# Differential stage: the second norm moved into the second values tile, wider spacing of a tile's steps, weight low halves that yield to two steps, and a swapped first output bank

## The reference, cut to what matters

```python
h = _rms(x, norm_g)                       # norm of the final-normed x: two norms in a row
q, k, v, g = split(h @ w_in)              # 8 heads of two 64-wide halves
qs = [_rope_partial(_rms(q[..., c, :], q_norm), pos) for c in range(2)]
ks = [_rope_partial(_rms(k[..., c, :], k_norm), pos) for c in range(2)]
a = probs(qs[0], ks[0]) - lam * probs(qs[1], ks[1])     # per block of 128 queries
o = _rms(a @ v, subln) * (1 - lambda_init) * silu(g)
return x + o @ w_out
```

## Time and profile before

| what | us |
|---|---|
| median of three runs | 2985.66 |
| the profiled execution | 2983.96 |
| its span, first to last instruction | 2982.0 |
| TensorE (matmul) busy | 2909.0 |
| VectorE busy | 1623.4 |
| ScalarE busy | 1069.4 |
| GpSimd busy | 391.2 |

### The profile page before, as it was taken

One profiled execution on the slowest core, in us unless ns is written; L12 is line 12 of the kernel. 1 busy time (PEld: TensorE's weight loads), 2 busy tenths in 40 slices (PEclk: granted clock), 3 DMA queues, 4 the chain that ended last, 5 costly groups with the idle time before them and its releaser, 6 DMA issues.

```text
span 2982.0 us, 35867 instructions
## 1 busy us (share of the span) xinstructions
PE 2909.0 (98%) x14832; PEld 2426.6 (81%) x14832; DVE 1623.4 (54%) x2239; ACT 1069.4 (36%) x1664; POOL 391.2 (13%) x262
## 2 busy tenths in 40 slices
PE   7999999999999999999999989999999999999999
PEld 6888888779888888888888879888888778678877
DVE  5554356565455533555346565555533666666774
ACT  4232234344333222323234444333223444434442
POOL 2000111120100001000011120100001312144330
PEclk8999999999999999999999999999999999999999
DMA  3333332233223323332332223333322222121211
GB/s 124 98 98 96 96 86 65 63 106 111 87 92 99 96 94 101 93 98 93 99 86 78 64 86 113 92 101 99 99 92 92 64 58 64 43 86 57 71 57 50
DMA packets 301361, 257.20 MB, mean 86 GB/s; under 512 B 10871, under 2 KB 299536, under 8 KB 301200
## 3 DMA queue, kind: packets, MB, share of 16 engines
q1 hardware_dynamic: 300880, 254.90, 27.9%
q0 software_dynamic: 320, 0.03, 0.0%
HBM read 252.79 MB, written 2.10 MB: 85 GB/s over the span
## 4 chain that ended last, share of the span: by engine, by line
PE 91%; DVE 5%; ACT 1%; issue 1%; POOL 1%; SPq 0%; DMA 0%; POOLq 0%; ACTq 0%; DVEq 0%
PE PS L1431 28%; PE PS L1433 28%; PE PS L1432 28%; PE PS L1673 2%; PE PS L1437 2%; DVE WL L2133 2%; PE PS L1678 1%; PE PS L1520 1%; PE PS L1629 1%; DVE PS L2393 0%; DVE AF L2548 0%; POOL SC L2658 0%; PE PS L1679 0%; DVE X L2395 0%; DVE SM L2466 0%
## 5 line engine op out<-in xcount | busy, mean ns | idle before, releaser
L2133 DVE TENSOR_TENSOR WL<-RAW,WH 128x1024 fp32r<-128x1024 f32 x480 | 624.0, 1306 | 583.9 <-ACT WH L1786 583.5
L1431 PE MATMUL PS<-XH,WL 128*128 128x512 f32 x2256 | 901.9, 400 | 9.0 <-issue 9.0
L1433 PE MATMUL PS<-XH,WH 128*128 128x512 f32 x2256 | 883.4, 392 | 0.0
L1432 PE MATMUL PS<-XL,WH 128*128 128x512 f32 x2256 | 882.4, 391 | 0.0
L1786 ACT ACTIVATE WH<-RAW 128x1024 fp32r<-128x1024 f32 x448 | 465.6, 1044 | 1036.7 <-PE PS L1433 1022.0
L1433 PEld LDWEIGHTS PS<-XH,WH 128*128 128x128 f32 x2256 | 425.6, 189 | 92.1
L1431 PEld LDWEIGHTS PS<-XH,WL 128*128 128x128 f32 x2256 | 426.7, 189 | 90.5 <-issue 9.7
L1432 PEld LDWEIGHTS PS<-XL,WH 128*128 128x128 f32 x2256 | 426.9, 189 | 81.6 <-issue 0.5
L1431 PE MATMUL PS<-AR,WL 128*128 128x512 f32 (+1 forms) x1216 | 465.6, 383 | 15.2 <-DVE X L2395 10.0
L1433 PE MATMUL PS<-AR,WH 128*128 128x512 f32 (+1 forms) x1216 | 462.0, 380 | 0.0
L1432 PE MATMUL PS<-AR,WH 128*128 128x512 f32 (+1 forms) x1216 | 461.4, 379 | 0.0
(11 more groups left out here) (244 smaller groups left out, 3067.1 us busy)
## 6 DMA issues: line engine op xcount, KB each, us to landing
RAW<-in_w_ffn_gu_dram SPq DMA_DIRECT2D x176, 512.0 KB, 3.5
RAW<-in_w_ffn_down_dram SPq DMA_DIRECT2D x80, 512.0 KB, 3.4
RAW<-in_w_mix_in_dram SPq DMA_DIRECT2D x48, 512.0 KB, 3.9
RAW<-in_w_xkv_dram SPq DMA_DIRECT2D x32, 512.0 KB, 3.4
RAW<-in_a_w_in_dram SPq DMA_DIRECT2D x32, 512.0 KB, 4.0
RAW<-in_w_mix_out_dram SPq DMA_DIRECT2D x16, 512.0 KB, 3.5
RAW<-in_w_xq_dram SPq DMA_DIRECT2D x16, 512.0 KB, 3.5
RAW<-in_w_xo_dram SPq DMA_DIRECT2D x16, 512.0 KB, 3.5
```

What stands on the lines that cost most here:

```text
L1431: pe.matmul(o, ll, rh, start=start, stop=False, skip_group_check=skip)
L1432: pe.matmul(o, lh, rl, start=False, stop=False, skip_group_check=skip)
L1433: return pe.matmul(o, lh, rh, start=False, stop=stop, skip_group_check=skip)
L2133: dve.tensor_tensor(l, raw_slot(n), F(h), ALU.subtract).then_inc(sg["wl"].up(n))
```

## The change

It orders the steps of the differential stage in another way; what is computed stays the same.

```diff
+        self.first = "drot", "dob"
...
-            self.later(10, "drot", k, "dr")
+            self.later(12, "drot", k, "dr")
             if w == "k":
-                self.later(12, "dkb", k, "dkb")
-            self.later(13, "dsin", k, "dsn", "dco")
+                self.later(13, "dkb", k, "dkb")
+            self.later(15, "dsin", k, "dsn", "dco")
             if w == "k":
-                self.later(15, "dkt", k, "dkt")
-            self.later(18, "dad", k, "dad", *(("dkm",) if w == "k" else ()), "eh")
-            self.later(22, "dlo", k, "el")
+                self.later(16, "dkt", k, "dkt")
+            self.later(20, "dad", k, "dad", *(("dkm",) if w == "k" else ()), "eh")
+            self.later(24, "dlo", k, "el")
...
-            self.later(11, "dot", ("o", t), "dot")
-            self.later(14, "dom", ("o", t), "dog", "dov", "oh")
-            self.later(19, "dol", ("o", t), "ol")
+            self.later(13, "dot", ("o", t), "dot")
+            self.later(16, "dom", ("o", t), "dog", "dov", "oh")
+            self.later(21, "dol", ("o", t), "ol")
...
         self.drain(self.flow(g))
+        g = self.flow(self.values(s, 1))
+        for _ in range(4):
+            next(g)
         self.add("norm2a", (s,), "na2", "ms2", "pw2", "ep2", "rcol2")
...
-        g = self.flow(self.values(s, 1))
         for _ in range(5):
             next(g)
         shape_up("q", 0)
...
             for c in range(2):
-                yield from self.tile(out[0], c, c, range(6))
+                yield from self.tile(out[0], 1 - c, c, range(6))
             yield from gated(7)
```

## The result

The change made the kernel slower: 2988.75 us, median of 22 runs (2985.96 to 2993.96), against 2983.81 for the kernel before in the same comparisons (2980.41 to 2986.68). The ratio is 1.0018, 95% interval 1.0012 to 1.0025. The forecast was 2982.3, a gain of 3.4 us. The result lies inside the range, but on the wrong side of no change.

The account below looks back on a forecast made before the run. TensorE, busy 2909.0 of 2982.0 us, was taken as the bound, so only its idle or slow time could be regained. Terms -3.9 - 1.5 + 3.9 - 1.9 = -3.4 us gave a median of 2982.3; range 2971.5 to 2989.5.

Parts of the forecast that it names:

- the half clock in rounds 1 and 3: Behind new waits of the scores for `dlo`, 1.3 and 1.2 us: chance one in three, 0.6 us each.
- the collision: Low half behind `drot` of q beside GpSimd's product: costs 0 to 1.1 us, taken as 0.4.
- the yield at the start: At k0 and q0, both low halves come only after `drot` of q0: 0.8 us gained.
- norm: Second norm's sums after four values steps: 1.4 us less idle, and a half clock worth 1.7 us gone.
- round 0: `dsq` wait of q1 stays; `drot` wait goes, 0.6 us; half of a 1.7 us half clock saved; together 1.5.
- rounds 1 and 2: Scores after round 1's `don`: -1.5 us from the later `dlo`, plus 0.6 for a half clock; -0.9.
- rounds 3 and 4: Scores after round 3's `don`: +0.1 us from the later `dlo`, plus 0.6 for a half clock; +0.7.
- round 5: Scores wait 3.2 us for `dlo`: +1.3 us, plus 1.6 for an almost certain half clock; +2.9.
- round 6 and opening: Round 6: later `dlo` and half clock, +1.2 us; opening: shorter or vanished waits of `dot` for `dob`, -1.9.
- `dlo` of q would be late: Rounds 1, 3, 5, 6: VectorE's longer queue ends `dlo` 20.5 us after `don` starts; head scores wait for it.
- Rival B: Rounds 1, 3, 5, 6: yielded low halves delay `dlo` to 22 us, half clock each; 2993.5 us, chance 0.12.
- The swap: First output tile's bank: 2.1 us wait and its half clock go, but `dlo` of q7 is awaited; within round 6's -0.4.

Follow-up runs that it names:

- `dsin` at 14 ticks: The changed kernel with `dsin` one tick earlier, so GpSimd's product of k comes ahead of the power of `don`: 2990.32 us, 1.0025.
- The norm alone: The kernel before with one edit, four values steps put ahead of the second norm's sums: 2978.15 us, ratio 0.9983.
- the kernel that doesn't yield: The changed kernel with `self.first` empty, so low halves no longer yield; wider steps, norm and bank swap stay: 2977.63 us, 0.9978.
- the old spacing: The changed kernel with the spacing of all steps as before; yielding low halves, norm and bank swap stay: 2973.64 us, 0.9967.
- the two pairs of kernels: Kernel before plus the norm's edit, with swap 2979.66 us, without 2978.15; old spacing, yield, norm, `dad` at 16, with swap 2971.41, without 2971.69.

## Why the prediction was wrong

The mechanism in the rounds was read right, and its prices were too low: the step that failed is the price of the half clock in rounds 1 and 3 (0.6 each in the sum, 3.2 measured), and beside it the collision (0.4, measured 1.08). A second step, the gain of 0.8 from the yield at the start, had the sign wrong. TensorE's starts in the two profiles give the shift (after less before) at each place, and with it each term:

| stretch | predicted | measured |
|---|---|---|
| up to `don` of round 1 (norm, low halves, round 0; -0.65 of it before the norm) | -5.4 | -0.6 |
| rounds 1 and 2 | -0.9 | +2.0 |
| rounds 3 and 4 | +0.7 | +3.7 |
| round 5 | +2.9 | +3.9 |
| round 6 and opening | -0.7 | +0.1 |
| after the stage | 0 | -1.4 |
| sum | -3.4 | +7.7 |

**Right.** Every order that the prediction derived stands in the trace: L2729 ahead of L2723 of k, two low halves behind `drot` of q, `dgb` and a low half ahead of `dlo`, `dkb` at 0.42 to 0.43 us in seven of its eight (k1's still takes 1.50). The waits that it said would go have gone. That `dlo` of q would be late was right, and nearly so by how much: 20.5 us forecast, 20.9 measured. In that closeness there is some luck. From `dad` of k on, 16.5 were forecast without the collision and 16.2 came, which hides 0.3 of the 0.7 by which the collision was too small; and `dsin` at 14 ticks shows that the start of `dad` of k, from which the sum counts, doesn't set the end.

**The half clock, the largest error.** The step was "I count a half clock with one chance in three in rounds 1 and 3 (0.6 each) and as good as certain in 5 and 6 (1.6 each)". It came in all four, and lasted 6.8 us, not 3.4. By the intervals above a stretch costs 3.2 in round 1 and 2.2 in round 5. Rounds 1 and 3 alone are 5.2 us above the 0.6 taken for each. With these prices and `dlo` 0.4 later the table's terms come out as 2.1 (rounds 1 and 2), 3.7 (3 and 4) and 3.9 (5), against 2.0, 3.7 and 3.9 measured. All stretches of this stage were 3.4 us long before, and I took that length for fixed. The rest of the same trace spoke against it: at the end of a wait of 3.21 us, ahead of the sums at 648.57, the granted clock falls to 0.50 for 6.8 us (the row is of before).

```profile
648.50:655.20 6.70, 6.63 (x20) 5.56 (x21) 4.68 (x6) 2.60 (x3) 1.04 (x2) 0.50 0.58 181
```

I had also read "three more waits of about 1 us are followed by none" as speaking against one here, where the waits forecast were 1.3 and 1.2; they came out at 1.8, and were followed.

**The collision.** "A collision costs between 0 and 1.1. I take 0.4." It is 1.08 in every round. Nothing in the rows was near 0.4; the orders that I had myself derived put the second low half beside the product each time. With 1.1 the sum would have been 2.8 higher, but only 1.6 of it was felt, the 0.4 a round by which `dlo` came later than forecast.

**The start.** "Both low halves now come only after `drot` of q0. I take 0.8 back." Behind `drot` of q0 they stand beside GpSimd's two products (VectorE took 4.54 us for the two), and `dad` of k0 and `dlo` of q0 come behind them: 1.21 us of wait for k1's bank, 1.87 at the first scores, and a stretch at half clock. The norm alone brought the first scores forward by 3.6 us, the whole change by 1.4. From the sums at 2308.7 to `don` of round 1 the profiles show against before: -3.1 us with the norm alone, -5.0 in the kernel that doesn't yield, -1.3 with the old spacing, and 0.0 in the changed kernel. So here too it is the yield with the wide spacing that takes the gain away. I asked what the low halves stood in front of where they were, and in the rounds where they would land, but not here.

**Rival B** (chance 0.12) was the mechanism that came, at 20.9 us of `dlo` and not the 22 that it assumed. It gave 2993.5, and "decides from about 21.3 us on". That point was too high, since it too counted a stretch at 1.7.

**Round 0, opening.** The wait of `dsq` stayed, and the half clock of 2368 too (1.7 was halved in the sum). The opening's waits went.

**The swap** was rightly put at nothing of its own: neither of the two pairs of kernels shows a gain.

## What to carry to other kernels

When work is told to yield, look up at every place what it then lands in front of, and what runs on GpSimd beside it there: a low priority that waits for one step stands at the head of the queue right behind it. Two edits that each remove the same wait should be timed alone and together; here neither lost alone and the pair did, because together they made the same queue longer. Where a new wait on TensorE is foreseen, put a stretch at half clock on its bill, 1.6 to 3.2 us here, by how often waits of that length had one (the table below), and keep its length open: in four rounds it was twice as long as any in this stage before. Look for lengths in the whole trace and not in one stage.

## What the runs showed of the hardware

Whether a wait of TensorE brings a granted clock of 0.50, and for how long, does not follow from the length of the wait. These are all waits of 0.9 us and more in this stage and just behind it, over the 13 profiles, by what they brought; two that began inside a stretch are left out:

| wait, us | no stretch | 3.4 us | 6.8 us |
|---|---|---|---|
| 0.9 to 1.2 | 27 | 6 | 0 |
| 1.2 to 1.7 | 10 | 12 | 1 |
| 1.7 to 2.2 | 3 | 6 | 5 |
| above 2.2 | 0 | 7 | 7 |

Longer waits bring a stretch more often, but 0.97 us brought one in round 1 of the kernel before, and 0.97 to 0.98 none in three other rounds, and 1.82 brought 6.8 us where 1.86 in another version brought none. In this stage the lengths are always one of the two. What decides stays open: no experiment varied the matmuls around a wait of one length.

The medians move by more than the queue does. Bringing `dlo` forward by 1.5 us in four rounds gave 10.5 us. The waits for it fell by 5.9; the profile also has 20.5 us less at half clock in this stage, and at the prices above that more than covers the rest.

How long an instruction on GpSimd shows in a profile can be mostly the wait for VectorE. A product over 8 columns took 0.20 us by itself and 1.12 when it started inside a low half, and one over 512 columns 1.30 and 2.20. The other way round, a low half of 1.22 us took 2.31 behind the long product and 1.22 behind the short one.
